# Compression and prompt attention of a hybrid decoder step: from one after the other to alternating on TensorE

## What is computed

```python
kc = _compress(kvc[:, :, 0], cmpk_pe, cmpk_w1, cmpk_b1, cmpk_w2)   # and vc from cmpv_*
# _compress: 16-row chunks; hid = gelu(ua[:, :-1] + ub[:, 1:] + b1); return hid @ w2
p_cmp = softmax(q_c . kc, chunks that have ended);  o_cmp = p_cmp . vc
score = sums of p_cmp by block of 64 rows; the first and the local blocks forced
idx   = top_k(score, 16)
o_slc = softmax(q_r . k of the chosen blocks) . v   # rows of a paged pool, for the sampled requests
o_win = softmax(q_r . k of the last 512 rows) . v
o     = gates[0] * o_cmp + gates[1] * o_slc + gates[2] * o_win
```

## Time and profile before

| what | us |
|---|---|
| median of three unprofiled runs | 2299.14 (2295.13 to 2305.86) |
| the profiled execution | 2298.58 |
| its span, first to last instruction | 2296.8 |
| TensorE busy | 2165.2 |
| VectorE busy | 788.2 |
| ScalarE busy | 444.7 |
| GpSimd busy | 364.6 |

### The profile page before, as it was taken

The page is one execution under the profiler, slowest core; times in us unless marked ns, Lnnn a source line. Parts: engine busy times, 40 slices in busy tenths (PEclk is TensorE's granted clock), DMA queues, the critical chain, the costliest instruction groups (busy, mean ns, idle before and its releaser), DMA issues.

```text
span 2296.8 us, 30286 instructions
## 1 busy us (share of the span) xinstructions
PE 2165.2 (94%) x12250; PEld 1739.6 (76%) x12250; DVE 788.2 (34%) x1649; ACT 444.7 (19%) x1014; POOL 364.6 (16%) x486
## 2 busy tenths in 40 slices
PE   6999996878999999999999999788899999999997
PEld 5789884546888888888887988644578888888886
DVE  3455326563332022022345623456624211211214
ACT  2331013223211011011224111222332111100111
POOL 2000212425110000000200022133421000000002
PEclk8999996879999999999999999878899999999998
DMA  9204432342242222222131053322312222222211
GB/s 278 75 1 139 147 124 107 114 140 87 83 124 74 74 68 70 74 74 74 51 79 32 20 193 119 148 111 103 91 30 73 83 74 73 68 71 74 74 37 45
DMA packets 246634, 205.22 MB, mean 89 GB/s; under 512 B 26808, under 2 KB 232352, under 8 KB 244064
## 3 DMA queue, kind: packets, MB, share of 16 engines
q1 hardware_dynamic: 231680, 126.13, 19.4%
q0 software_dynamic: 14816, 77.15, 9.2%
HBM read 197.09 MB, written 14.48 MB: 92 GB/s over the span
## 4 chain that ended last, share of the span: by engine, by line
PE 85%; DVE 8%; issue 2%; ACT 2%; SPq 2%; POOL 0%; DMA 0%; DVEq 0%; ACTq 0%
PE ps L377 71%; PE ps L497 5%; PE ps L498 5%; PE ps L558 2%; DVE ar L1918 1%; PE ps L546 1%; DVE ov L1693 1%; DVE ps L1864 1%; ACT ov L1384 1%; SPq L925 1%; SPq L917 0%; DVE wr L1918 0%; DVE ov L1705 0%; PE ps L586 0%; DVE ts L1545 0%
## 5 line engine op out<-in xcount | busy, mean ns | idle before, releaser
L377 PE MATMUL ps<-hT,wr 128*128 128x272 f32 x2304 | 540.1, 395 | 7.6 <-DMA wr<-in_w_in 6.9
L377 PEld LDWEIGHTS ps<-hT,wr 128*128 128x128 f32 x2304 | 440.3, 191 | 100.2 <-DMA wr<-in_w_in 7.3
L377 PE MATMUL ps<-hT,ar 128*128 128x272 f32 x1792 | 417.2, 393 | 0.8 <-ACT ov L1316 0.6
L377 PEld LDWEIGHTS ps<-hT,ar 128*128 128x128 f32 x1792 | 340.1, 190 | 72.2 <-issue 2.4
L377 PE MATMUL ps<-ov,wr 128*128 128x272 f32 x1024 | 240.7, 392 | 0.0
L377 PEld LDWEIGHTS ps<-ov,wr 128*128 128x128 f32 x1024 | 193.9, 190 | 39.5
L2030 DVE TENSOR_SCALAR ov<-ov,par 128x560 f32<-128x560 f32 x48 | 27.4, 571 | 458.0 <-ACT ov L1479 437.7
L377 PE MATMUL ps<-ov,ar 128*128 128x272 f32 x768 | 180.1, 393 | 2.0 <-DVE hT L1906 2.0
L377 PEld LDWEIGHTS ps<-ov,ar 128*128 128x128 f32 x768 | 145.5, 190 | 32.1 <-issue 2.4
L497 PE MATMUL ps<-ar,w 128*128 128x256 f32 (+1 forms) x576 | 166.1, 370 | 0.0
L498 PE MATMUL ps<-ar,w 128*128 128x256 f32 (+1 forms) x576 | 164.7, 367 | 0.0
(11 more groups left out here) (314 smaller groups left out, 2243.5 us busy)
## 6 DMA issues: line engine op xcount, KB each, us to landing
wr<-in_ffn_w_in SPq DMA_DIRECT2D x53, 512.0 KB, 3.7
ar<-in_ffn_w_in SPq DMA_DIRECT2D x43, 512.0 KB, 3.7
wr<-in_ffn_w_down SPq DMA_DIRECT2D x27, 512.0 KB, 4.1
ar<-in_ffn_w_down SPq DMA_DIRECT2D x21, 512.0 KB, 4.1
ar<-in_cache_win_kv POOLq DMA_DIRECT2D x4, 2048.0 KB, 8.6
out_s_win<-in_cache_win_kv SPq DMA_DIRECT2D x16, 508.0 KB, 7.8
wr<-in_w_in SPq DMA_DIRECT2D x14, 512.0 KB, 3.6
ar<-in_w_in SPq DMA_DIRECT2D x12, 512.0 KB, 3.6
```

The source lines that it names most:

```text
L377: mm = lambda o, a, b, st, sp: nc.tensor.matmul(o, a, b, start=st, stop=sp)
```

## The change

One list now orders compression and attention together. The prompt's compression unit becomes the third of nine. The list starts with the six products of units 0 to 2. Then step n puts the scores of prompt unit n in front of one further product, for n = 0 to 11, and each unit's second layer stands behind the next unit's first product. The sampled requests start 13 steps later than before, with the same spacing; the spreading of their queries over partitions is moved from the head of the attention to step 12, and their compressed scores to steps 5 to 7 and 12 to 14. All other engines take their parts from the same list, so that on GpSimd the cache loads now alternate with the prompt's weighing, on ScalarE the Gelu with the Exp, and on VectorE the chunk transposes with the maxima.

To have banks for both at once, products use bank 7 alone, and second layers and compressed scores move to banks 4 and 5, which turns, probabilities and outputs share with them. The prompt's values now open the accumulation of a tile's output, ahead of the compressed branch. The mask moves from the compression's weights to weight slot 4, and that slot's output weights wait for the last maximum. Three waits in front of the attention are moved to the instructions that need them.

```diff
-        mask_row = lambda i: free1[:, 3104 + 384 - i * P:3104 + 512]
+        mask_row = lambda i: wr_flat[:, 4096 + 384 - i * P:4096 + 512]
...
-        compressed_units = lambda l: [(l, "cmp", x) for x in range(DB - 1)] + [(l, "cmpp", 0), (l, "cmp", DB - 1)]
+        compressed_units = lambda l: [(l, "cmp", 0), (l, "cmp", 1), (l, "cmpp", 0)] + [(l, "cmp", x) for x in range(2, DB)]
...
-        BASE = (0, 2, 6, 9, 11, 15)
+        BASE = (13, 15, 19, 22, 24, 28)
         SAMPLE_PARTS = {"keys": -1, "scores0": 0, "scores1": 1, "turn": 2, "values": 3, "output": 4}
-        CMP_PARTS = {4: ("scores", 0), 5: ("group", 0), 6: ("values", 0), 8: ("scores", 1)}
+        CMP_AT = {5: ("scores", 0), 6: ("group", 0), 7: ("values", 0), 12: ("scores", 1), 13: ("group", 1), 14: ("values", 1)}
         plan = []
-        for n in range(-1, NU + 3):
+
+        def compress_piece(x, v):
+
+            plan.append(("cmp", "product", (x, v)))
+            if x and v == 0:
+                plan.append(("cmp", "second", x - 1))
+
+        for x in range(3):
+            for v in range(2):
+                compress_piece(x, v)
+        for n in range(max(NU + 3, BASE[-1] + 5)):
             if 0 <= n < NU:
                 plan.append(("prompt", "scores", n))
+            if n < 12:
+                compress_piece(3 + n // 2, n % 2)
+            if n == 12:
+                plan.append(("cmp", "second", DB))
+                plan.append(("sample", "spread", (0, 0, None)))
...
-            if n == 0:
-                plan.append(("sample_cmp", "group", 1))
+            if n in CMP_AT and CMP_AT[n][0] != "values":
+                plan.append(("sample_cmp", *CMP_AT[n]))
...
-            if n == 1:
-                plan.append(("sample_cmp", "values", 1))
+            if n in CMP_AT and CMP_AT[n][0] == "values":
+                plan.append(("sample_cmp", *CMP_AT[n]))
...
+            if 0 <= n - 3 < NU:
+                plan.append(("prompt", "values", n - 3))
...
-            if 0 <= n - 3 < NU:
-                plan.append(("prompt", "values", n - 3))
...
-                                   "three": ((4, 5, 7), "three", 1), "out": ((6,), "out", 1)}[kind]
+                                   "three": ((4, 5), "three", 1), "product": ((7,), "product", 1), "out": ((6,), "out", 1)}[kind]
...
-                    hb = take((u, "hid", v), "acc")
+                    hb = take((u, "hid", v), "product")
...
-                    b = take((l, i, "O"), "out")
+                    b = S.bank_of[l, i, "O"]
                     pe.wait_ge(sem("copied_v"), after("copied_v", (l, i, "c")))
+                    pe.wait_ge(sem("vbd_built"), after("vbd_built", l))
...
-                b = take((l, "qrep"), "two")
-                pe.wait_ge(sem("qbd_built"), after("qbd_built", l))
-                for c in range(4):
...
+                def spread_queries():
+                    b = take((l, "qrep"), "two")
+                    pe.wait_ge(sem("qbd_built"), after("qbd_built", l))
...
+                product = compress()
+                us = compressed_units(l)
                 for who_, what, n in plan:
-                    if who_ == "sample":
+                    if what == "product":
+                        product(us[n[0]], n[1])
+                    elif what == "second":
+                        compress2(us[n])
+                    elif what == "spread":
+                        spread_queries()
+                    elif who_ == "sample":
...
-                    b = take((l, G, "Scs"), "quad")
+                    b = take((l, G, "Scs"), "three")
...
-                compress(l, compressed_units(l))
-                pe.wait_ge(sem("kT_copied"), after("kT_copied", (l, "w")))
-                pe.wait_ge(sem("q_roped"), after("q_roped", (l, 3)))
-                pe.wait_ge(sem("vbd_built"), after("vbd_built", l))
                 prompt_attention(l)
...
-                if 0 <= n - unit_no[l, "out", 0] < NW and n % NW != 4:
+                if 0 <= n - unit_no[l, "out", 0] < NW and n % NW == 4:
+                    sp.wait_ge(sem("neg_max"), after("neg_max", (l, NU - 1)))
+                elif 0 <= n - unit_no[l, "out", 0] < NW:
...
-                po.wait_ge(sem("projected"), after("projected", (l, "kv", "c1")))
-                cache(l * A0 + NCMP + NA)
-                po.wait_ge(sem("compressed"), after("compressed", (compressed_units(l)[-1], 1)))
+                for w in range(unit_no[l, "out", 0] - NW, unit_no[l, "out", 0]):
+                    if w % NW == 4:
+                        for s, n_ in freed(("w", w)):
+                            po.wait_ge(s, n_)
                 nc.gpsimd.memset(mask_row(3)[:, 0:384], 0.0).then_inc(sem("mask_ready"), up("mask_ready"))
+                po.wait_ge(sem("tables_loaded"), after("tables_loaded", 0))
                 nc.gpsimd.tensor_copy(mask_row(0), cst[:, K_CAUS:K_CAUS + P]).then_inc(sem("mask_ready"), up("mask_ready", l))
...
                 for who_, what, n in plan:
-                    if (who_, what) == ("prompt", "weigh"):
+                    if what == "product" and n[1] == 0:
+                        cache(l * A0 + n[0] + 2)
+                    elif (what, n) == ("second", DB):
+                        cache(l * A0 + NCMP + NA)
+                    elif (who_, what) == ("prompt", "weigh"):
                         weigh(n)
                     elif (who_, what) == ("sample", "values"):
                         cache(l * A0 + NCMP + (4, 6, 8, 9, 9, 9)[n[0]])
...
-                for i, u in enumerate(us):
-                    compress(u, us[i - 1] if i else (l - 1, "cmp", DB - 1) if l else None)
-                    if CMP_PARTS.get(i, ("", 0))[0] != "scores":
-                        continue
-                    G = CMP_PARTS[i][1]
+
+                def sample_weights(G):
...
+                    if n == 0:
+                        ac.wait_ge(sem("kv_stored_c"), after("kv_stored_c", l))
+                    if n == 2:
+                        ac.wait_ge(sem("compressed2"), after("compressed2", (us[2], 1)))
                     ac.wait_ge(sem("neg_max"), after("neg_max", (l, n)))
...
                 for who_, what, n in plan:
-                    if who_ == "sample":
+                    if what == "product":
+                        x, v = n
+                        hidden_layer(us[x], v, us[x - 1] if x else (l - 1, "cmp", DB - 1) if l else None)
+                    elif what == "spread":
+                        copy_spread()
+                    elif (who_, what) == ("sample_cmp", "scores"):
+                        sample_weights(n)
+                    elif who_ == "sample":
                         sample_part(what, *n)
...
-                for x, u in enumerate(us):
-                    if x:
-                        second_layer(us[x - 1])
-                    if x + 2 < len(us):
-                        turn_chunks(us[x + 2])
-                    if x == len(us) - 1:
-                        second_layer(u)
-                    if x in CMP_PARTS:
-                        sample_cmp(*CMP_PARTS[x])
-
...
                 ve.wait_ge(sem("mask_ready"), after("mask_ready", l))
                 for who_, what, n in plan:
-                    if who_ == "sample":
+                    if what == "product":
+                        if n[1] == 0 and 0 < n[0] < DB:
+                            turn_chunks(us[n[0] + 1])
+                    elif what == "second":
+                        second_layer(us[n])
+                    elif what == "spread":
+                        copy_spread()
+                    elif who_ == "sample":
                         sample_part(what, *n)
```

## The result

| | before | after |
|---|---|---|
| median of the unprofiled runs | 2299.05 us | 2352.25 us (2347.75 to 2352.59) |
| ratio, 95% interval | 1 | 1.0224 (1.0196 to 1.0251) |
| span of the profiled execution | 2296.8 us | 2346.0 us |
| TensorE busy | 2165.2 us | 2175.5 us |
| ScalarE busy | 444.7 us | 501.2 us |

The forecast of 2348 us was 4 us off. In the profiled executions the loss lies where it was put: 24.2 and 24.5 us in the two attention stages, nothing elsewhere (the next layer's first product follows the output projection after 777.1 us in both traces). The profiled execution after took 2347.75 us, the shortest of the four; the other three took 2352.0 to 2352.6, and no trace shows where their 4 to 5 us lie.

What follows compares the result with a forecast made beforehand. TensorE was taken to bound the compression, and a chain of six dependent sampled units to stretch over 197 of the attention's 212 us. Terms sum to 366.5 for 342.2 us per layer, 48 more in two: 2348 us, range 2302 to 2384.

Steps and rivals of the forecast that it cites:

- (a): Prelude of each layer: six products before any prompt unit, with three waits for a Gelu; 40.5 us.
- (b): Twelve steps mixing products with prompt units: 126 us of work plus 13 of small waits, 139 us.
- (c): Step 12: last second layer, spread queries, second sampled scores and a Gelu wait; 7 us.
- (d): Steps j = 0 to 12, counted from the first sampled scores: 128 us, bounds 115 and 140, for 139.3 before.
- (e): Steps j = 13 to 19, last two sampled pairs without prompt units: 47 us, bounds 39 and 55, for 58.1 before.
- (f): Output projection starting at the lower clock after a sparse tail: 5 us lost, bounds 0 and 6.
- rival with the product's single bank: Every mixed product waits 2 us more because its Gelu queues behind an Exp block: 2396 us, chance 0.10.
- I let these two cancel: In j = 0 to 12: 11 us of relief taken as offset by fewer transient banks and three of four compressed tiles.
- the chain stays as long: Summary: prompt units' TensorE work comes ahead of the sampled chain, not in its gaps; 24 us more per layer.
- long key step: Sampled step where VectorE transposes two key blocks ahead of a copy TensorE awaits; forecast to stay at 15 to 20 us.
- interleaving pays: Rival: the sampled chain shortens with half the prompt work off VectorE's order; 2269 us, chance 0.08.
- the change doesn't interleave: Rival: the prompt chain doesn't fit into two steps, each mixed step takes 17.6 us; 2492 us, chance 0.03.

Runs made afterwards that it cites:

- e9: Changed kernel with all products first, no prompt unit among them, and still two transient banks behind them: 2362.3 us, ratio 1.0275 to the kernel before.
- e10: Changed kernel with all products first, no prompt unit among them, and the third transient bank given back behind them: 2300.5 us, ratio 1.0002 to the kernel before.
- e6: Changed kernel, still 12 units among the products, with bank 7 given back as third transient bank behind them: 2340.6 us, ratio 1.0166 to the kernel before.
- e12: Changed kernel with three transient banks, sampled units set later: twelve mixed units, ten prompt units alone, then the sampled chain alone: 2372.7 us, ratio 1.0313.
- e11: Changed kernel with 4 units among the products, three transient banks and a pair's key blocks in different steps: 2256.6 us, ratio 0.9812 to the kernel before.
- e8: Kernel before the change with the two key blocks of a sampled pair transposed in different steps, nothing else: 2273.7 us, ratio 0.9882.
- e3: Changed kernel with 8 instead of 12 prompt units among the products, two transient banks: 2372.0 us, ratio 1.0313 to the kernel before.

## Why the prediction was right, point by point

| term, layer 0 | predicted | measured |
|---|---|---|
| (a) six products | 40.5 | 43.1 |
| (b) twelve mixed steps | 139 | 143.9 |
| (c) step 12 | 7 | 7.3 |
| (d) j = 0 to 12 | 128 | 129.9 |
| (e) j = 13 to 19 | 47 | 42.3 |
| (f) cold projection | 5 | 0 |
| sum | 366.5 | 366.5 |

The sum is exact by luck: errors of +9.7 and -9.7 met. It is also that of the shortest of the four executions; by the medians the change cost 53 us, some 5 more than the sum says. The direction is no luck: the moved work came ahead of the sampled steps, and these (j = 0 to 19) fell only from 197.4 to 172.2 us, for the 175 forecast.

(a) The three waits came as computed (1.89 and twice 0.61, for 2.2 and twice 0.75): the first is what the row of the table load gave, with nothing more behind the load. What was missing is what the first does to the clock; that is told below. The prompt unit's load was covered, as said.

(b) The waits are 10.2 us for the 13 taken; work is 133.7 for 126, some of it at the lower clock behind waits of 2.72 and 2.85 us (clock 0.96). The rival with the product's single bank has no support: TensorE's waits for a Gelu in layer 0 are these, and three of the four lie in the products ahead.

```profile
PE ps L512 <- ACT hid L1278: 3.9, 4, 1.9
```

(c) Right. The first sampled scores came at 414.4 us for the 408 forecast, mostly by what (a) and (b) ran over.

(d) Right in size, and the weakest in reason. "I let these two cancel" set 11 us of relief against the missing bank, whose price I could not read from the trace of before, since there the third bank bridges the waits. e9 and e10 price it at 27.6 us per layer where all units stand in the chain, e6 at up to 6.7 where twelve are gone. So (d) came out by luck too: two terms that no row of before could price met. The same holds for the summary "the chain stays as long": with three banks a moved unit gives back 3.4 of its 5.2 us, and with two banks as much as it costs, so that the summary is the cause of 40 of the 52 us only if the units are counted first and the bank second. The long key step did stay, 19.0 us, and splitting the keys showed that it was worth shortening.

(e) Too long by 4.7: the last pair's scores, 64 matmuls, took 8.39 us, near full clock, where I had 12 at partly half clock. That is 3.6 of it.

(f) Wrong. The projection started at full clock (581.15, 8 matmuls in 2.07 us, as in the earlier trace rows). The mechanism exists: in e12 the same projection, behind a chain with nothing beside it, began at the lower clock. Mis-sized even there: (3.96 - 2.07) + (2.92 - 2.00) = 2.8 us, not 5.

```profile
592.26 3.96 PE L395 MATMUL ps<-ov,ar 128*128 128x272 f32 x8 [1.82 <-DVE hT L2018]
596.02 2.92 PE L395 MATMUL ps<-hT,ar 128*128 128x272 f32 x8
598.78 2.00 PE L395 MATMUL ps<-ov,wr 128*128 128x272 f32 x8
```

The rival "interleaving pays" lost for twelve units; e11 shows a part of what it expected, sampled steps 8.2 us shorter than in e8. That the change doesn't interleave is refuted by the mixed steps' 12.0 us each. Left open: whether the bank has any price in the kernel after (0 to 12 us), and why eight units (e3) came out slower than twelve in the median; its spread of 2358 to 2376 is the widest of all.

## What to carry to other kernels

When independent work is moved out of a dependent chain's gaps to stand ahead of it, count what it costs there against what the chain gives back for each piece: the pieces that stand alone at the end are gained, those that fill a gap are lost, and a handful may then be the best (here 4 of 22, of the counts 0, 4 and 12 that were compared). A buffer taken from a rotation is priced by what the rotation bridges, not by the waits that the old trace shows, and give it back as soon as its other user is through. Look in the longest steps for one engine's block that stands ahead of a copy others wait for; splitting it won more than its own time.

## What the hardware did that I had not expected

The same wait, in the same place of the same instruction order, moved the clock in one execution and not in another. In three kernels TensorE waits 1.89 and then 0.61 us for the first two Gelus among the six products ahead; the stretch took 43.1 us at a mean clock of 0.96 in the kernel after, 47.7 at 0.85 in e6 and 41.4 at 1.00 in e12. Behind the first wait the clock fell in the kernel after and in e6, and not in e12; in e6 it fell once more behind a wait of 0.61 us ahead of the prompt's own product. The first of these is the first window shown of the kernel after; those of e6 and e12:

```profile
215.20:262.90 47.70, 44.52 (x209) 38.51 (x208) 8.10 (x13) 4.21 (x8) 9.72 (x12) 0.85 0.36 120
```

```profile
213.70:255.10 41.40, 38.07 (x209) 32.72 (x208) 8.10 (x13) 4.21 (x8) 9.72 (x12) 1.00 0.42 137
```

So 6.3 us of a stretch of 42 can come and go with the clock alone, and two profiled executions can't be compared more finely than that in such a stretch. Second, ScalarE's 44 further table loads (1058 for 1014 instructions) made it 56.5 us busier, 1.28 each, and TensorE waited for its Gelus 3.9 us in a layer.
